# Projection of the gated half in 512- and 256-column matmuls summed by VectorE, and the final scaling shared with GpSimd

## The reference

```
def _sgu_mixer(h, w_in, v_gain, w_s, b_s, w_out):
    z = _gelu(h @ w_in)
    u, v = z[..., :SGU_WIDTH], z[..., SGU_WIDTH:]
    v = _rmsnorm(v, v_gain)...
    sv = jnp.einsum('gpq,bnqgd->bnpgd', w_s, v) + b_s.T[:, :, None]
    return (u * sv.reshape(bsz, length, SGU_WIDTH)) @ w_out
...
    return _rmsnorm(x_lat, final_gain)
```

## Time and profile before

| | us |
|---|---|
| median of 3 runs (lowest, highest) | 1839.95 (1839.45, 1843.02) |
| the profiled execution | 1840.57 |
| its span, first to last instruction | 1838.8 |
| TensorE busy | 1822.3 |
| VectorE busy | 1514.9 |
| ScalarE busy | 965.1 |
| GpSimd busy | 452.4 |

### The profile page before, as it was taken

How to read it: one execution, slowest core, us unless ns; L and a number is a source line. 1 busy time by engine, 2 the same in 40 slices (tenths; PEclk the granted TensorE clock), 3 DMA queues, 4 the chain that set the end, 5 groups by cost and what they waited for, 6 DMA issues and landing times.

```text
span 1838.8 us, 35135 instructions
## 1 busy us (share of the span) xinstructions
PE 1822.3 (99%) x11712; PEld 1582.2 (86%) x11712; DVE 1514.9 (82%) x2803; ACT 965.1 (52%) x1616; POOL 452.4 (25%) x225
## 2 busy tenths in 40 slices
PE   8999999999999999999999999999999999999998
PEld 7999988888888888888889998888888888888887
DVE  6775889989998888888878589997999888885555
ACT  6654455655555444445554545565555544445554
POOL 6046588950000000000000368893000000000000
PEclk9999999999999999999999999999999999999999
DMA  9866455556554555588874455555655455555553
GB/s 383 330 236 221 161 184 192 184 199 217 202 178 165 182 172 175 186 310 319 322 263 154 158 170 185 190 185 206 217 194 171 170 174 174 180 172 190 194 191 133
DMA packets 104182, 376.40 MB, mean 205 GB/s; under 512 B 12464, under 2 KB 12464, under 8 KB 103856
## 3 DMA queue, kind: packets, MB, share of 16 engines
q1 hardware_dynamic: 103392, 373.37, 58.4%
q0 software_dynamic: 432, 2.10, 0.3%
q10 hardware_dynamic: 288, 0.06, 0.0%
HBM read 374.43 MB, written 1.05 MB: 204 GB/s over the span
## 4 chain that ended last, share of the span: by engine, by line
PE 85%; DVE 6%; DMA 5%; ACT 2%; POOL 1%; issue 0%; SPq 0%; ACTq 0%; DVEq 0%; POOLq 0%
PE ring L1845 19%; PE O L1902 13%; PE O L1904 12%; PE O L1903 12%; PE ring L1843 5%; PE ring L1850 5%; DMA raw<-in_u 3%; PE ring L1807 3%; PE ring L1550 2%; PE ring L1551 2%; PE ring L1552 2%; ACT wH L560 2%; DVE wL L931 2%; PE ring L1833 2%; PE ring L1812 1%; PE O L1833 1%
## 5 line engine op out<-in xcount | busy, mean ns | idle before, releaser
L560 ACT ACTIVATE wH<-raw 128x1024 fp32r<-128x1024 f32 x597 | 633.3, 1061 | 794.0 <-DMA raw<-in_v 361.3
L931 DVE TENSOR_TENSOR wL<-raw,wH 128x1024 fp32r<-128x1024 f32 x384 | 470.2, 1225 | 171.6 <-ACT wH L560 166.6
L1845 PE MATMUL ring<-hX,wH 128*128 128x512 f32 x1984 | 482.8, 393 | 0.0
L1845 PEld LDWEIGHTS ring<-hX,wH 128*128 128x128 f32 x1984 | 362.1, 188 | 69.6 <-issue 1.1
L1902 PE MATMUL O<-wH,gateH 128*128 128x512 f32 x1024 | 402.2, 393 | 0.2
L1904 PE MATMUL O<-wH,gateL 128*128 128x512 f32 x1024 | 399.0, 390 | 0.0
L1903 PE MATMUL O<-wL,gateH 128*128 128x512 f32 x1024 | 398.6, 389 | 0.0
L520 POOL TENSOR_TENSOR wL<-raw,wH 128x1024 fp32r<-128x1024 f32 x128 | 322.0, 2524 | 46.5 <-ACT wH L560 45.5
L1904 PEld LDWEIGHTS O<-wH,gateL 128*128 128x128 f32 x1024 | 192.2, 188 | 40.8
L1902 PEld LDWEIGHTS O<-wH,gateH 128*128 128x128 f32 x1024 | 192.3, 188 | 39.7 <-DVE gateL L1431 0.6
L1903 PEld LDWEIGHTS O<-wL,gateH 128*128 128x128 f32 x1024 | 192.4, 188 | 39.0
(11 more groups left out here) (219 smaller groups left out, 2408.6 us busy)
## 6 DMA issues: line engine op xcount, KB each, us to landing
raw<-in_u SPq DMA_DIRECT2D x256, 512.0 KB, 3.2
raw<-in_v SPq DMA_DIRECT2D x256, 512.0 KB, 3.2
ada_v<-in_ada SPq DMA_DIRECT2D x40, 512.0 KB, 4.4
raw<-in_w_q SPq DMA_DIRECT2D x30, 512.0 KB, 3.3
ada_m<-in_ada SPq DMA_DIRECT2D x24, 512.0 KB, 5.1
raw<-in_w_in SPq DMA_DIRECT2D x23, 512.0 KB, 4.2
ada_f<-in_ada SPq DMA_DIRECT2D x16, 512.0 KB, 15.1
raw<-in_w_out SPq DMA_DIRECT2D x16, 512.0 KB, 3.6
```

Of the source, the lines that this page charges most:

```text
L560: nc.scalar.activation(wH[s % RAW][:, :], (place or raw[s % RAW])[:, :], ACT.Copy).then_inc(s_h, 1)
L931: nc.vector.tensor_tensor(wL[s % RAW][:, :], raw[s % RAW][:, :], wH[s % RAW][:, :].bitcast(fp32), ALU.subtract).then_inc(s_low, 1)
L1845: ins = mm(bank[:, :], wH[s][:, k * P:k * P + P], hX[:, k, :, :].rearrange("p two t -> p (two t)"), start=(not low_weights_first and k == ...
```

## The change

In w_u each tile is made in the form of the query projection: 8 matmuls of 512 columns and then 8 of 256 into the bank. ScalarE copies the right half to UV, VectorE adds the left half to it, and ScalarE takes gelu of UV in place, one loop step later. The bank is freed by VectorE's addition. At the end, VectorE scales 6 of the 8 tiles and SyncE sends them in three pairs; GpSimd multiplies the other two by the gain as soon as the residual is there, TensorE spreads the factor a second time, into O[3], ScalarE copies it to SBUF, GpSimd multiplies, and ScalarE issues these two DMAs.

```diff
@@ -203,6 +203,8 @@
         s_gates = [sem(f"s_gates{x}") for x in range(6)]
         s_front = [sem(f"s_front{x}") for x in range(16)]
         s_half = sem("s_half")
+        s_gate_hl = sem("s_gate_hl")
+        s_gate_sum = sem("s_gate_sum")
         s_hl = sem("s_hl")
         s_sum = sem("s_sum")
         s_query = sem("s_query")
@@ -235,6 +237,9 @@
         s_rooted = sem("s_rooted")
         s_xn = sem("s_xn")
         s_hf = sem("s_hf")
+        s_hf_p = sem("s_hf_p")
+        s_gained = sem("s_gained")
+        s_spread = sem("s_spread")
         s_hH = sem("s_hH")
         s_hin = sem("s_hin")
         s_vc = sem("s_vc")
@@ -298,6 +303,8 @@
                        (ws[:, :, :], ws_d)]
         BIAS, SMALL = 16 * len(bias_loads), 16 * len(small_loads)
         NORMS = 2 * LAYERS + 1
+        BY_DVE = 6
+        gained, spread_out = UV[:, 0:KT - BY_DVE, :], UV[:, KT - BY_DVE, :]
 
 
         ADA_FRONT, ADA_U0, ADA_V0, ADA_U1 = 2 * KT, 5 * KT, 6 * KT, 11 * KT
@@ -470,10 +477,10 @@
                 with sp.Fori(done // 4, tiles // 4) as i:
                     for s in range(4):
                         load(src, base, i, s)
-            for p in range(4):
+            for p, (lo, hi) in enumerate(((0, 2), (2, 4), (4, BY_DVE))):
                 sp.wait_ge(s_hf, p + 1)
-                sp.dma_start(out_d[:, 2 * p:2 * p + 2, :], hf[:, 2 * p:2 * p + 2, :]).then_inc(s_out, 16)
-            sp.wait_ge(s_out, 64)
+                sp.dma_start(out_d[:, lo:hi, :], hf[:, lo:hi, :]).then_inc(s_out, 16)
+            sp.wait_ge(s_out, 80)
 
 
         @block.gpsimd
@@ -550,6 +557,14 @@
                     pool.wait_ge(s_pe, BASE["v", 0] + 116)
                     pool.dma_start(keys[:, 0], k1_d[1]).then_inc(s_late, 16)
                     pool.dma_start(keys[:, 1], k2_d[1]).then_inc(s_late, 16)
+            for k in range(BY_DVE, KT):
+                pool.wait_ge(s_res, KT * (LAYERS - 1) + k + 1)
+                nc.gpsimd.tensor_scalar(gained[:, k - BY_DVE, :], XT[:, k, :], fg[:, k:k + 1], None, ALU.mult)\
+                    .then_inc(s_gained, 1)
+            pool.wait_ge(s_gained, KT - BY_DVE)
+            pool.wait_ge(s_spread, 1)
+            for k in range(BY_DVE, KT):
+                nc.gpsimd.tensor_tensor(hf[:, k, :], gained[:, k - BY_DVE, :], spread_out, ALU.mult).then_inc(s_hf_p, 1)
 
 
         @block.scalar
@@ -672,6 +687,10 @@
                         tokens_squared(g)
                         split_high(W_U, 0, g)
                     tokens_out(3)
+                    def gate_gelu(t):
+                        act.wait_ge(s_gate_sum, t + 1)
+                        nc.scalar.activation(UV[:, t, :], UV[:, t, :], ACT.Gelu).then_inc(s_bank_a, 1)
+
                     for t in range(16):
                         ahead(W_U, t // 4, t % 4)
                         if t == 0:
@@ -679,10 +698,13 @@
                             act.wait_ge(s_ssq, 1)
                             nc.scalar.activation(vstd[:, :], ssum[:, :], ACT.Sqrt, bias=eps[:, :], scale=1.0 / SGU_W)\
                                 .then_inc(s_vstd, 1)
+                        if t:
+                            gate_gelu(t - 1)
                         act.wait_ge(s_pe, W_U + t + 1)
-                        nc.scalar.activation(UV[:, t, :], ring[t % 4][:, 0:T], ACT.Gelu).then_inc(s_bank_a, 1)
+                        nc.scalar.activation(UV[:, t, :], ring[t % 4][:, T:2 * T], ACT.Copy).then_inc(s_gate_hl, 1)
                         for f in HIGH_AT.get(t, ()):
                             gated_high(f, f + 1)
+                    gate_gelu(15)
                     gated_high(14, 15)
                     ahead(W_OUT, 0, 0)
                     gated_high(15, 16)
@@ -896,6 +918,11 @@
                 if layer < LAYERS - 1:
                     ahead(base, 31, 3)
                 norm(2 * layer + 2)
+            act.wait_ge(s_rstd, NORMS + 1)
+            nc.scalar.activation(spread_out, O[3][:, 0:T], ACT.Copy).then_inc(s_spread, 1)
+            for lo, hi in ((BY_DVE, BY_DVE + 1), (BY_DVE + 1, KT)):
+                act.wait_ge(s_hf_p, hi - BY_DVE)
+                act.dma_start(out_d[:, lo:hi, :], hf[:, lo:hi, :]).then_inc(s_out, 16)
 
 
         @block.vector
@@ -994,10 +1021,10 @@
                 inverse_root(n)
                 dve.wait_ge(s_rstd, n + 1)
                 if n == NORMS - 1:
-                    for k in range(KT):
+                    for k in range(BY_DVE):
                         ins = nc.vector.scalar_tensor_tensor(hf[:, k, :], XT[:, k, :], fg[:, k:k + 1], O[2][:, 0:T], ALU.mult,
                                                              ALU.mult)
-                        if k % 2:
+                        if k % 2 or k == BY_DVE - 1:
                             ins.then_inc(s_hf, 1)
                     return
                 scaled(n, 0)
@@ -1114,9 +1141,15 @@
                         nc.vector.tensor_tensor(gL[:, f, :], UV[:, SGU_FT + f, :], gH[:, f, :].bitcast(fp32),
                                                 ALU.subtract).then_inc(s_gL, 1)
 
+                    def gate_sum(t):
+                        dve.wait_ge(s_gate_hl, t + 1)
+                        nc.vector.tensor_tensor(UV[:, t, :], ring[t % 4][:, 0:T], UV[:, t, :], ALU.add).then_inc(s_gate_sum, 1)
+
                     for t in range(16):
                         if t < 14:
                             ahead(W_U, t // 4, t % 4)
+                        if t:
+                            gate_sum(t - 1)
                         if t in U_ADA:
                             ada_early(m)
                             m += 1
@@ -1141,6 +1174,7 @@
                             gate_by(t - 2)
                         for f in LOW_AT.get(t, ()):
                             gated_low(f)
+                    gate_sum(15)
                     gate_by(14)
                     gated_low(12)
                     gate_by(15)
@@ -1552,6 +1586,16 @@
                     ins = mm(bank[:, 0:T], b, xH[:, k0 + k, :], start=False, stop=(last and k == KT - 1))
                 ins.then_inc(s_pe, 1)
 
+            def wide_gate(t):
+
+                pe.wait_ge(s_l0, W_U + t + 1)
+                for k in range(KT):
+                    mm(ring[t % 4][:, :], wH[t % RAW][:, k * P:k * P + P], hX[:, k, :, :].rearrange("p two t -> p (two t)"),
+                       start=(k == 0), stop=False)
+                for k in range(KT):
+                    ins = mm(ring[t % 4][:, 0:T], wL[t % RAW][:, k * P:k * P + P], hH[:, k, :], start=False, stop=(k == KT - 1))
+                ins.then_inc(s_pe, 1)
+
             def first_tiles(base, n, emptied, before, count):
 
                 def high(t, k):
@@ -1721,15 +1765,18 @@
                         gate_block(3, s, 0)
                         gate_block(3, s, 1)
                     for t in range(16):
-                        pe.wait_ge(s_bank_a, (6, 8, 10, 12)[t] if t < 4 else 16 + t + 1)
-                        tile_product(W_U, t // 4, t % 4, ring[t % 4], hH, hL)
+                        if t < 4:
+                            pe.wait_ge(s_bank_a, (6, 8, 10, 12)[t])
+                        else:
+                            pe.wait_ge(s_gate_sum, t - 3)
+                        wide_gate(t)
                         for f in MIX_AT.get(t, ()):
                             mix_tile(f)
                     for t in range(2 * KT):
                         i, s = t // 4, t % 4
                         j, kk = 2 * i + s % 2, s // 2
                         if t < 2:
-                            pe.wait_ge(s_bank_a, 4 + 16 + 13 + t)
+                            pe.wait_ge(s_gate_sum, 13 + t)
                         if kk == 0:
                             pe.wait_ge(s_bank_v, j + 1)
                         tile_product(W_OUT, i, s, ring[j % 4], gH, gL, KT * kk, first=(kk == 0), last=(kk == 1),
@@ -1942,7 +1989,9 @@
                 if layer == 0:
                     keep_clock(4, O[3])
                 spread(2 * layer + 2)
-                if layer == 0:
+                if layer == LAYERS - 1:
+                    spread(2 * layer + 2, O[3])
+                else:
                     keep_clock(6, O[3])
 
 
```

## The result

The changed kernel took 1844.45 us (median of 22 runs), the kernel before, in runs beside it, 1841.48 us. The ratio is 1.0016, with a 95% interval of 1.0010 to 1.0022: 2.9 us slower, 1.8 to 4.1. (One of the 22 took 5658.89 us; the ratio leaves it out, and the median of the other 21 is 1844.32.) The forecast was +1.7 us. The profiled execution took 1843.50 us, with a span of 1841.7.

A forecast was written before the change was run, and what follows sets the result against it. The prediction took TensorE's successive instructions and its waits as the bound. Terms -0.2 (w_u), +2.7 (hand-off) and -0.8 (end) sum to +1.7 us, giving 1841.7 us as the median, range 1838.6 to 1845.6.

The forecast's parts named there:

- rival A: Hand-off to w_out: remainder 15 misses GpSimd's pause, TensorE waits 5.1 us, total 1844.1 us; chance 0.22.
- Matmuls, -1.3: In w_u, tiles take 2.79 instead of 2.87 us, gaining 1.3 us over 16 tiles.
- the issue gap: In w_u, alternative estimate from the skill's N/2.4 + 2.5 ns: 0.02 us a tile, 0.3 in all, ending at 1842.7.
- VectorE's additions in w_u, +1.1: In w_u, one VectorE addition per tile delays remainders TensorE needs: 0.7 us of waits early, 0.4 at tile 11.
- Near tile 4: In w_u, late mixing weights and remainder 4 make TensorE wait 0.7 us; tile 4 starts at about 76.65, not 76.28.
- At tile 11: In w_u, VectorE's lead is used up; remainder 11 is done at 100.1, TensorE arrives at 99.7, costing 0.4 us.
- The hand-off, +2.7: From w_u to w_out, gating remainders fall among GpSimd's long operations; TensorE waits 2.7 us from 124.9.
- gating 14 stands behind the addition and misses GpSimd's start: At w_u's end, gating 14 follows tile 15's addition until 119.4, GpSimd has started, and everything follows one or two slots later.
- The end, -0.8: In the last microseconds, VectorE scales 6 tiles instead of 8, so the last output DMA goes 0.8 us earlier.
- B (no wait): Hand-off to w_out: the slots don't matter and the second output waits for nothing, total 1839.0 us; chance 0.19.
- D: At the end, GpSimd's products come late: +0.3 us there, total 1842.8; chance 0.52 together with the forecast.
- Rival C (the clock): After a 4 to 5 us wait at the hand-off, the granted clock falls to 1.2 GHz: 2.4 us more, 1846.5; chance 0.07.

The follow-up runs named there:

- wide alone: Kernel before with only the wide matmuls in w_u, nothing added on VectorE, one product left out of the result: ratio 1.0012.
- the repeat: The changed kernel run again without alteration, for a second profile, against the kernel before: ratio 1.0020.
- gating 14 first: Changed kernel with VectorE's gating of row 14 put ahead of the addition of tile 15: ratio 1.0004 against the kernel before.
- end alone: Kernel before with only the change's last part, the split final scaling, w_u as before: ratio 0.9999.
- addition alone: Kernel before with its 256-column matmuls, plus ScalarE's copy, one VectorE operation per tile and gelu one tile later: ratio 1.0008.
- the hold: Changed kernel, GpSimd waiting for all 16 gating remainders before its first 1024-column remainder: ratio 0.9994 against the kernel before; the same wait was added to other versions.
- pause: Changed kernel, GpSimd waiting for 12 gating remainders ahead of the remainder of w_out's third tile: ratio 1.0019 against the kernel before.
- the two holding versions: GpSimd waits for all 16 gating remainders, in the changed kernel (0.9994) and with w_u changed but the end as before (0.9993), against the kernel before.
- before, hold: Kernel before, with GpSimd waiting for all 16 gating remainders before its first 1024-column remainder: ratio 0.9997.

## Why the prediction came out as it did

The sign and the class (within 0.2%) came as forecast, the time inside the range; the size was too small by 1.2 us (+1.7 forecast, +2.9 measured, 1.8 to 4.1). The time itself, 1844.45, is nearest to rival A's 1844.1, and that is chance: 1.5 us of the distance to the forecast's 1841.7 is that the kernel before stands at 1841.48 here and not at the 1839.95 of three runs. Point by point:

- **Matmuls, -1.3: right.** 2.79 us a tile, and the wide matmuls alone shorten the stage by 1.2 to 1.3 us (51.94 and 52.06 against 53.23). The estimate that the issue gap of the Trainium skill (TensorE: Matmul & The Clock Gate, Back-to-back issue gap) led to, 0.3 us, is refuted by this.
- **VectorE's additions in w_u, +1.1: right on the whole, one term wrong.** The eight profiles with both wide matmuls and additions have a mean stage of 52.94 us against 53.18 of the three with neither: -0.24, forecast -0.2. Near tile 4 the loss is 0.9 in the repeat (tile 3 to tile 4 takes 4.60 us instead of 3.69), forecast 0.7. At tile 11 it is 0.2 (tile 10 to tile 11 takes 2.98 us, 96.97 to 99.95, instead of 2.79), forecast 0.4: remainder 11 begins 2.9 us later than before in the repeat (98.59 for 95.66), where I had put 4.4. The first delay is 0.6 us (remainder 4 at 75.18 for 74.58), not 1.0, and seven additions follow it, not ten. A third error hid these two: 95.66 and 4.4 make 100.1, which is when the remainder would begin; it would be done 1.23 later, and the term would have been 1.6. That it came out near is luck.
- **The hand-off, +2.7: right in size, wrong in reason.** The lock and the price of a long operation were right, as was a remainder that slips into GpSimd's pause (14, where I had 15); 2.4 us of waits, and the stretch 2.4 to 2.8 us longer. The step that does not hold is "gating 14 stands behind the addition and misses GpSimd's start". In the profiles the wait stays with gating 14 first, is 0.2 us with the additions alone, and comes with the wide matmuls alone; and in the changed kernel GpSimd has no pause near 118.5 whose end gating 14 could miss. I had carried GpSimd's times over from the profile before and moved VectorE only. Shorter tiles free buffers earlier, w_out's tiles arrive earlier, ScalarE splits them earlier (115.80 instead of 117.38 with the wide matmuls alone), and GpSimd follows; VectorE, held at every short operation of GpSimd, does not. My own row had the hint: that split had waited 2.88 us for its DMA, and I took from it only that GpSimd might start later. Moving VectorE was not wrong in itself. In the two profiles with the tiles of before and neither additions nor hold, GpSimd's first long operation starts at 122.03 and 121.61 and remainder 13 at 120.51 and 120.97; in the three with the whole change in w_u, it is 120.71, 121.43 and 121.20, and 120.92, 121.64 and 121.41. So GpSimd is 0.2 to 1.3 us earlier and VectorE up to 1.1 later. How much of the wait is due to each is not shown.
- **The end, -0.8: wrong.** The ends of the range were -0.8 and +0.3; "end alone" shows none of it. GpSimd's products took 0.7 us each (1837.02, 1.41 for two), ScalarE and GpSimd were in time, and the last DMA was issued 2.5 us behind the first scaling instead of 3.25. But from that issue to the span's end it is 3.2 us, where it was 2.5. The term was read from the issue of the last DMA, with its landing taken as unchanged. The rows of the DMA engines above point to the reason: what fills the time is the transfer of the 1.05 MB, some 3 us, and its start hangs on the first issue, which is 0.90 us behind the first scaling in both kernels. Only the last issue had moved. A version with an earlier first issue was not run.
- **Rival A (5.1 us of wait)** is in no profile; **B (no wait)**, of the profiles with wide matmuls, only in those with the hold. **D** (+0.3 at the end) didn't come: the end is as before.
- **Rival C (the clock)** had the right mechanism, the wrong condition and the wrong price. I tied it to a wait of 4 to 5 us. It came with 2.3 us in the repeat and 1.8 us in "wide alone", where TensorE had 0.29 us of work from 124 to 126; and it did not come in "pause", with a wait of 2.7 us and no work from 124 to 126. The stretch is then longer by 1.4 us more (50.81 and 51.22 against 49.38 to 49.78). Seen by whole executions, the mean clock reads 0.998 instead of 0.999 or more in 11 of the 32 compared executions of the changed kernel and in 8 of 11 of "wide alone", in 2 of 103 of the kernel before and in none of 44 with the hold; "addition alone" has 2 of 11, which its one profile does not explain. The changed kernel's runs at 0.998 have a median 1.4 and 2.0 us above those at 0.999 of their group (1845.3 and 1843.9; 1846.5 and 1844.5). The repeat's own profiled execution, with the fall, reads 0.999 all the same, so 11 is a lower count.

The sum by what was measured: -0.2 for the stage, +2.4 to +2.8 at the hand-off, 0 at the end, and +1.4 to 2.0 in at least a third of the executions, some +0.6 on the average: +2.8 to +3.2, against +2.9. That the two spans differ by 2.9 us as well is partly chance: at the first load of the keys the difference is 1.1 us (165.2 for 164.1), the other 1.8 arise behind it. From there to the end the fourteen profiles take between 1672.5 and 1677.5 us, with nothing changed but the last microseconds, so a single pair of profiles can't carry a difference of 1 us.

What stays open: what decides in an execution whether the clock falls after such a wait, why "gating 14 first" is timed lower and "addition alone" higher than their profiles say, and how the wait divides between GpSimd's earlier and VectorE's later start. Whether the hold makes the change pay is not settled either: the two holding versions, 0.9994 and 0.9993, have intervals that just include 1, and "before, hold" stands at 0.9997.

## What to carry to other kernels

Where an engine that shares something with another is made ready earlier, ask who does not come earlier with it: here a gain of 1.3 us on the bounding engine moved GpSimd's long operations over VectorE's last ones and cost 2.4 us and more. Read the whole chain of buffers behind a shortened stage (load, split, remainder) before carrying times over from the old profile. And where two engines exclude each other, one wait that keeps the long operations back until the short ones are through costs next to nothing if their results aren't due (TensorE waits at most 0.5 us for GpSimd up to w_out's end with the hold, 0.4 in the kernel before), and took 4 us off the changed kernel (1.0016 to 0.9994). Last, where several transfers end a kernel, look at when the first can start and how long the bytes take, and not only at the last issue.

## What the runs showed of the hardware

- A VectorE operation with two SBUF operands takes 0.41 us alone, 0.96 beside GpSimd's 256-column operations and up to 2.65 beside its 1024-column ones; the addition with one operand in PSUM takes 0.41 to 0.43, also inside GpSimd's run (0.41 at 118.27).
- Where the last remainders sat through two long operations, TensorE's last wait (1.85 to 2.7 us) was followed by 3 us at a granted clock of 0.50 (1.2 of 2.4 GHz) in two profiles and by 1.00 in four. The Trainium skill (TensorE: Matmul & The Clock Gate, Part 1) says that idle time may halve the clock; the two profiles with the fall agree, though no row here tells the waits with a fall from those without.
- Issuing the last output DMA 0.8 us earlier brought 0.1 us (5.75 to 5.7): with the first issue where it was, the 16 DMA engines took some 3 us for the 1.05 MB either way.
